# Four heads of a DeltaNet stage as hardware loops on four engines, and one product of the modulation rows moved a level earlier

## The reference

```python
for i in range(DEPTH):                                   # DEPTH = 2
    ada = (silu(c) @ ada_w[i] + ada_b[i])[:, None, :]
    sh1, sc1, g1, sh2, sc2, g2 = jnp.split(ada, 6, axis=-1)
    h = rms_norm(x) * (1.0 + sc1) + sh1
    y = gdn_mixer(h, ...) if i % 2 == 0 else fox_mixer(h, ...)
    x = x + g1 * y
    h = rms_norm(x) * (1.0 + sc2) + sh2
    x = x + g2 * hier_moe(h, ...)
return rms_norm(x, final_norm)
```

```python
u = triangular_solve(a_mat, v * beta)
w = triangular_solve(a_mat, kb * exp(g))
v_new = u - w @ S;  o = qg @ S + qk @ v_new;  S = S * exp(g_last) + kd.T @ v_new
```

## Time and profile before

| | |
|---|---|
| median of three runs | 1527.34 us |
| the profiled execution | 1527.44 us |
| its span, first to last instruction | 1525.7 us |
| PE busy | 1389.7 us, 91% of the span |
| DVE, ACT, POOL busy | 724.8, 433.8, 406.5 us |
| mean granted TensorE clock | 0.959 of full speed |
| instructions | 25390 |

### The profile page before, as it was taken

One profiled execution on the slowest core, in us unless ns is written; L12 is line 12 of the kernel. 1 busy time (PEld: TensorE's weight loads), 2 busy tenths in 40 slices (PEclk: granted clock), 3 DMA queues, 4 the chain that ended last, 5 costly groups with the idle time before them and its releaser, 6 DMA issues.

```text
span 1525.7 us, 25390 instructions
## 1 busy us (share of the span) xinstructions
PE 1389.7 (91%) x9319; PEld 917.6 (60%) x9319; DVE 724.8 (48%) x1486; ACT 433.8 (28%) x1017; POOL 406.5 (27%) x595
## 2 busy tenths in 40 slices
PE   4999999999999898999988699999999989999881
PEld 2877777777887554555544377767774455555440
DVE  3565555555565246732222525555555466422224
ACT  4334244244334220000000645555543110000002
POOL 3142022021023001434332333444420013443320
PEclk8799999999999998999999899999999989999996
DMA  8244644643016237999999522111118279999995
GB/s 352 103 169 163 221 169 164 222 166 111 1 56 235 84 128 280 418 418 418 420 418 415 208 78 76 70 69 69 69 69 317 83 260 411 421 417 420 419 399 196
DMA packets 56694, 350.30 MB, mean 230 GB/s; under 512 B 18408, under 2 KB 18880, under 8 KB 30992
## 3 DMA queue, kind: packets, MB, share of 16 engines
q1 hardware_dynamic: 44992, 332.02, 54.8%
q0 software_dynamic: 11520, 16.83, 3.0%
q10 hardware_dynamic: 80, 0.04, 0.0%
HBM read 342.45 MB, written 27.34 MB: 242 GB/s over the span
## 4 chain that ended last, share of the span: by engine, by line
PE 73%; DMA 13%; DVE 8%; ACT 3%; issue 2%; SPq 0%; ACTq 0%; POOL 0%; DVEq 0%; POOLq 0%
PE PS L1000 10%; PE PS L752 8%; DMA hT<-in_moe_w_down_dram 8%; PE PS L754 7%; PE PS L753 7%; PE PS L943 5%; PE PS L1007 5%; DMA Dr<-in_ada_w_dram 3%; PE PS L835 3%; PE PS L854 3%; PE PS L723 3%; PE PS L851 3%; PE PS L1027 2%; PE PS L1017 2%; PE PS L1176 2%
## 5 line engine op out<-in xcount | busy, mean ns | idle before, releaser
L752 PE MATMUL PS<-hHi,Whi 128*128 128x512 f32 x512 | 228.4, 446 | 0.7 <-DVE hLo L1652 0.7
L754 PE MATMUL PS<-hHi,Wlo 128*128 128x512 f32 x512 | 203.3, 397 | 0.0
L1242 ACT COPY arena<-PS 128x512 f32<-128x512 f32 (+3 forms) x256 | 112.3, 458 | 318.3 <-PE PS L835 162.7
L753 PE MATMUL PS<-hLo,Whi 128*128 128x512 f32 x512 | 202.4, 395 | 0.0
L1000 PE MATMUL PS<-Wr,arena 128*64 128x256 f32 x1408 | 166.3, 390 | 9.8 <-DVE arena L2013 9.8
L1000 PEld LDWEIGHTS PS<-Wr,arena 128*64 128x64 f32 x1408 | 102.0, 141 | 89.4 <-issue 29.6
L2225 POOL TENSOR_TENSOR Wlo<-Wr,Whi 128x512 fp32r<-128x512 f32 (+1 forms) x80 | 104.7, 1326 | 188.5 <-ACT Whi L1242 187.5
L1446 ACT ACTIVATE arena<-PS 128x128 f32<-128x128 f32 x72 | 20.0, 277 | 468.9 <-PE PS L1000 378.5
L2280 POOL DMA_INDIRECT y_rows<-arena x72 | 76.8, 1067 | 261.8 <-DVE arena L2025 255.5
L752 PEld LDWEIGHTS PS<-hHi,Whi 128*128 128x128 f32 x512 | 97.9, 191 | 31.9 <-issue 17.9
L754 PEld LDWEIGHTS PS<-hHi,Wlo 128*128 128x128 f32 x512 | 97.5, 190 | 22.4
(11 more groups left out here) (362 smaller groups left out, 2424.3 us busy)
## 6 DMA issues: line engine op xcount, KB each, us to landing
Wr<-in_moe_w_gate_up_dram SPq DMA_DIRECT2D x52, 2048.0 KB
Dr<-in_ada_w_dram SPq DMA_DIRECT2D x42, 1024.0 KB, 26.9
Dr<-in_moe_w_down_dram SPq DMA_DIRECT2D x28, 1024.0 KB
arena<-in_moe_w_gate_up_dram SPq DMA_DIRECT2D x14, 2048.0 KB
hT<-in_moe_w_down_dram SPq DMA_DIRECT2D x26, 1024.0 KB
Wr<-in_gdn_w_dram SPq DMA_DIRECT2D x8, 2048.0 KB, 7.8
Wr<-in_fox_w_dram SPq DMA_DIRECT2D x8, 2048.0 KB, 7.9
shift_scale<-in_moe_w_down_dram SPq DMA_DIRECT2D x12, 1024.0 KB
```

The costliest lines, as they stand in the source:

```text
L752: mm(out_ap, a_hi, b_hi, start=(k == 0), stop=False)
L753: mm(out_ap, a_hi, b_lo, start=False, stop=False)
L754: return mm(out_ap, a_lo, b_hi, start=False, stop=(k == KD - 1))
L1242: return nc.scalar.copy(dst, src)
```

## The change

On PE, ACT and DVE the unrolled pair of iterations becomes a hardware loop of two iterations, and on POOL a hardware loop of three. ACT and DVE tell their `Link` of it. Thresholds of waits and some addresses that depended on the head are now computed in registers. Besides, the tuple of `ada_parts` puts part 3 into level 2 (with part 2), and parts 4, 5 and 6 one level earlier; level 6 keeps part 7 alone. That holds for all five heads, the unrolled head 0 too.

```diff
@@ PE, delta @@
                     if with_ada:
-                        ada_parts(d, (None, (0, 1), (2,), (3,), (4,), (5,), (6, 7))[l])
+                        ada_parts(d, (None, (0, 1), (2, 3), (4,), (5,), (6,), (7,))[l])
@@ PE @@
             step(1, 1)
-            for j in range(2):
+            with pe.Fori(0, 2) as j:
                 step(j * 2 + 2, 0)
                 step(j * 2 + 3, 1)
             step(6, 0)
@@ ACT @@
             step(1, 1, 2)
-            for j in range(2):
+            with act.Fori(0, 2) as j:
+                link.enter(j, 6)
                 step(j * 2 + 2, 0, j + 2)
                 step(j * 2 + 3, 1, j + 3)
+                link.leave(2)
             step(6, 0, 4)
@@ DVE @@
             delta(0, 1, 0)
-            for j in range(2):
+            with dve.Fori(0, 2) as j:
+                link.enter(j, 2 * (4 + 3 * (CONV - 1)))
                 delta(j * 2 + 1, j * 2 + 2, 1)
                 delta(j * 2 + 2, j * 2 + 3, 0)
+                link.leave(2)
             delta(H - 3, H - 2, 1)
@@ POOL @@
             delta(0, 1, 0)
-            for j in range(3):
+            with pool.Fori(0, 3) as j:
                 delta(j * 2 + 1, j * 2 + 2, 1)
                 delta(j * 2 + 2, j * 2 + 3, 0)
```

## The result

The changed kernel takes 1547.07 us (median of four runs, 1538.45 to 1548.21), the kernel before beside it 1525.62 us (four runs, 1519.82 to 1527.44). The ratio is 1.0125, with a 95% interval of 1.0088 to 1.0161; a second measurement gave 1543.53 against 1525.46 us, 1.0118 [1.0092, 1.0145]. By the two ratios the change makes the kernel 18 to 19 us slower; the two medians of the first measurement alone lie further apart, by 21 us. The times of the changed kernel spread widely: the 21 executions listed with it go from 1534.58 to 1551.24 us, with a median of 1543.23. The prediction said +6.3 us and a range up to 1539; all three medians lie above it.

What follows compares the result with a forecast made beforehand. The prediction took PE's own work to bound the DeltaNet stage and so the kernel. Part 3's stalls +7.0, part 7's gone -1.5, loops +0.8 gave +6.3 us, 1533.6 us, with a range of 1526.5 to 1539.

Steps and rivals of the forecast that it cites:

- PE bounds the stage: DeltaNet stage: PE's own work bounds each head, so an idle microsecond of PE is a microsecond of the kernel.
- Part 3 in level 2, +7.0 us: Level 2, heads 0 to 4: PE waits for part 3's weights, 1.4 us a head, 7.0 us in all.
- Part 7: Level 6: part 7 alone no longer waits for its weights; stalls of 0.33 (head 3) and 1.17 us (head 4) go, -1.5.
- Part 4 has 1.2 us of margin only because PE lost time in level 2: Level 3: part 4's weights land at 164.8, PE asks at 166.0; the margin exists only through the level 2 stall.
- The loops of DVE, ACT and POOL, hidden: Added register instructions, at most 0.45 us before L823, hidden by about 0.75 us; 0 to 0.1 us a head in the state chain.
- The turn of PE's loop: PE's branch back after head 2: costs nothing, as in the FoX loop; all loops together 0.8 us, from 0 to 4.
- the turn misses its code: Rival, chance 0.17: at the loop's turn PE stops once for 1 to 3 us; +2 to +5 on top, 1537 us.
- The stalls lower the clock: Rival, chance 0.08: each of five stalls brings a half-clock stretch costing 1.7 us, +8.5 in all, 1542 us.
- Code is fetched less: Mechanism of the faster rival: second iteration fetches no PE code, so loads of parts 2 and 3 land up to 0.5 us earlier.
- The sign of being wrong: DeltaNet heads: the prediction is wrong in its core if heads keep 57.3 us or a head takes over 59.5.
- The rival "faster": Chance 0.10: fewer code fetches (-1), part 7's stalls gone (-1.5) and a run like 1519.82 give about 1521 us.
- The sum: Whole kernel: +7.0 - 1.5 + 0.8 = +6.3 us on 1527.44 us, predicted 1533.6 us; this forecast's chance 0.50.

Runs made afterwards that it cites:

- the short loop: Kernel before with only PE's DeltaNet loop, the projection's two small products left out inside it (body 1580 instructions instead of 1836): 1497.14 us, one run.
- the shifted kernel: Kernel before with only the new tuple of parts, plus 128 instructions of fulfilled waits on PE before head 0: 1544.99 us, ratio 1.0135.

## Why the prediction was wrong, step by step

- **PE bounds the stage.** Right: the idle time that the edits add to PE is found in the length of the heads. One reading was incomplete: PE also waits 0.47 us for ACT's copy in front of L835 in level 1 of each head, where the prediction says that nothing but the parts is waited for in the levels.
- **Part 3 in level 2, +7.0 us.** Right. Forecast 1.4 a head; alone it adds 1.42 and 1.72 to heads 1 and 2, with waits of 1.24 to 1.41. With -1.5 for part 7 the forecast of the order was +5.5, measured +6.3. In the changed kernel head 4 has 2.69 us in place of 1.4.
- **Part 7.** The waits went as said; the saving of 1.5 was right for the new order, where part 7 replaces part 3 as a group by itself.
- **Part 4 has 1.2 us of margin only because PE lost time in level 2.** Right: without the stall of 1.35 the margin would be -0.15 us, and with the stall taken away part 4 waits 0.13 and 0.16 us in heads 0 and 1.
- **The loops of DVE, ACT and POOL, hidden.** Right, 0.9995; L823 has no wait. What is left, 0.1 us a head, stands in front of L835 (0.55 us for 0.47).
- **The turn of PE's loop.** This is the step that failed: "A turn costs PE nothing, because its sequencer runs ahead of the array", with 0.8 us for all loops in the sum. The smooth turns of the FoX loop do not carry over to a body of 1836 instructions. I had this as a rival, "the turn misses its code", at 0.17, with the stop "nearer 2 to 3" us and 1 hidden. The runs show 6.7 us of branch, 3.1 hidden, 3.9 to 4.0 idle, and 1.7 more for the clock behind it. The Trainium skill's page "Runtime: NRT & Kernel Launch", section "Instruction fetch mechanics", says that a taken branch whose target is outside the current window of two blocks stalls until the target is fetched, and gives PE room for 2048 instructions. The stall is as the rule says; the window is not, since bodies of 1499 and 1649 instructions, far longer than two blocks, turned in 0.22 us, and the limit came below the 2048, between 1649 and 1755. The loop, within a block of those 2048, deserved far more than 0.17. By the times the turn and what comes with it cost 5.0 us (PE's loop alone) to 7.6 (all loops, 1.0045, against the loops without PE's, 0.9995), where the sum had 0.8. The new order and the loops, measured apart, add up to 11 to 13 us, about 1537 to 1539 us, still inside the range; the rest of the miss is under "The sum".
- **The stalls lower the clock.** Half right. Single waits of 1.2 to 1.4 us did not lower it, as with the 0.97 us of the earlier trace rows. The idle time of about 4 us at the turn did in all four profiles that have it. Between lie waits that did (2.71, 2.50, 1.75 and 1.43 close together, 0.83 and 1.42, and in the short loop 1.90 to 2.25 and 1.0 in each of four heads) and others that did not (2.69, 2.25, 2.04, 1.94, 1.13 and 1.68, 1.27 and 1.37, 1.07 and 1.37). The length of the idle time alone does not decide it.
- **Code is fetched less.** It is fetched more, 16 blocks for 14.
- **The sign of being wrong.** The prediction named a head over 59.5 us as a sign that its core is wrong. Heads 3 and 4 of the changed kernel take 66.05 and 60.30.
- **The rival "faster".** Its "about 1521" does not come out of its own terms: 1519.82 - 1 - 1.5 + 0.8 is 1518 without the stalls of part 3, and 1525 with their 7.0.
- **The sum.** Beyond the turn, the whole costs 5 to 8 us more than its parts measured alone. No part of the prediction had such a term. What the runs support is this: the new order leaves parts 2 and 3 without slack, PE's loop moves the moments at which its code is fetched, a fetch as a load is issued comes with a late load, and the longer waits can pull the clock down. That a fetch makes a load late is shown by the shifted kernel for one head and by coincidence in the others. That the excess needs both edits is argued and not shown: its size is hardly above the noise of the times, and of two profiles of the changed kernel one has no excess and one stretch at half clock in these heads, the other 8.0 us and four. Its cause stays open to that extent.

## What to carry to other kernels

Count the instructions of a loop's body on PE before rolling it up: a short loop that turns for nothing says nothing about a long one, and here the price of one missed turn was 5 to 6 us, with the clock, as much as all the waits that the new order added. Where a bounding engine reads weights by DMA with less than a microsecond to spare, look at the small transfers as well: here blocks of 16 KB of the engine's own code came with late loads. Work that waits for a load gains nothing from standing earlier if its load does not start earlier too. And when the parts of a change do not add up, profile the whole more than once before explaining the rest: here two executions of one kernel gave two answers.

## What the hardware showed that I had not expected

- A taken branch on PE took 0.22 us with bodies of 795 to 1649 instructions, 3.6 to 4.3 us at 1755 and 1819 (FoX stage), and 6.7 to 6.8 us at 1836 (DeltaNet stage). The first block's packet started 1.0 us after the branch in the FoX stage and 4.3 to 4.5 us after it in the DeltaNet stage, where the DMA engines were full of data.
- A block of code fetched as a load of 1 MB is issued came with a wait for that load in 15 of 19 cases, in none of 51 without it (13 of the 19 are head 3).
- 128 instructions that only wait on long fulfilled semaphores have records of 0.05 us each but follow each other 0.11 us apart; in one place they took 13.7 us, of which the products queued ahead hid under 3, and PE was idle for 11.0.
